# A two-layer network on one core: the second mixer's attention gets a fourth buffer of weights, and its first head's weights are scaled by a product of two tensors

## The reference, cut to what matters

```python
p = masked_softmax(jnp.einsum('bqghd,bgqkd->bghqk', qb, kg) * scale, mask)     # selected
p = masked_softmax(jnp.einsum('bqghd,bkgd->bghqk', qb, kb) * scale, mask)      # window
o = gate[..., 0:1] * heads(o_cmp) + gate[..., 1:2] * heads(o_sel) + gate[..., 2:3] * heads(o_win)
return (o.reshape(B, S, NSA_INNER) * jax.nn.silu(z)) @ w_out
```

## Time and profile before

| | |
|---|---|
| median of 3 runs | 1896.23 us |
| profiled execution, its own time | 1899.72 us |
| its span | 1898.0 us |
| busy: PE, PE's weight loads | 1824.1 us (96%), 1484.7 us (78%) |
| busy: DVE, ACT, POOL | 1095.2 us, 675.3 us, 308.9 us |
| attention stage in the trace | from 626.1 to about 775.6 us |

### The profile page before, as it was taken

The page is one execution under the profiler, slowest core; times in us unless marked ns, Lnnn a source line. Parts: engine busy times, 40 slices in busy tenths (PEclk is TensorE's granted clock), DMA queues, the critical chain, the costliest instruction groups (busy, mean ns, idle before and its releaser), DMA issues. The chain is left out here.

```text
span 1898.0 us, 36850 instructions
## 1 busy us (share of the span) xinstructions
PE 1824.1 (96%) x15870; PEld 1484.7 (78%) x15870; DVE 1095.2 (58%) x1644; ACT 675.3 (36%) x1100; POOL 308.9 (16%) x292
## 2 busy tenths in 40 slices
PE   8999999999999788999999899999999999999997
PEld 6877757688888567778888669888878888888886
DVE  4664354553257788444366887778574635354545
ACT  4334332332223577442222374433233322122342
POOL 4210011130002565320021240000001000000011
PEclk9999999999999899999999999999999999999998
DMA  5334323142223010134421100002042322322221
GB/s 191 103 111 134 136 83 133 45 190 101 90 74 111 35 37 12 49 109 138 137 102 56 48 2 4 4 3 70 4 178 92 104 104 89 111 89 89 78 100 45
DMA packets 42848, 160.87 MB, mean 85 GB/s; under 512 B 5312, under 2 KB 14528, under 8 KB 28096
## 3 DMA queue, kind: packets, MB, share of 16 engines
q1 hardware_dynamic: 28480, 143.84, 22.1%
q10 hardware_dynamic: 14208, 14.68, 2.2%
HBM read 140.42 MB, written 16.78 MB: 83 GB/s over the span
## 5 line engine op out<-in xcount | busy, mean ns | idle before, releaser
L257 DVE TENSOR_TENSOR wlo<-raw,whi 128x2048 fp32r<-128x2048 f32 (+2 forms) x113 | 251.0, 2221 | 179.2 <-ACT whi L248 178.8
L248 ACT ACTIVATE whi<-raw 128x2048 fp32r<-128x2048 f32 (+2 forms) x113 | 209.0, 1850 | 320.8 <-PE ps L283 161.4
L281 PE MATMUL ps<-act_hi,whi 128*128 128x512 f32 x616 | 243.1, 395 | 0.0
L301 PE MATMUL ps<-act_lo,whi 128*128 128x512 f32 x632 | 242.7, 393 | 0.0
L283 PE MATMUL ps<-act_hi,wlo 128*128 128x512 f32 x616 | 240.6, 391 | 0.0
L282 PE MATMUL ps<-act_lo,whi 128*128 128x512 f32 x616 | 240.5, 390 | 0.0
L300 PE MATMUL ps<-act_hi,whi 128*128 128x512 f32 x592 | 236.4, 399 | 0.0
L305 PE MATMUL ps<-act_hi,wlo 128*128 128x512 f32 x632 | 156.5, 389 | 0.0
L301 PEld LDWEIGHTS ps<-act_lo,whi 128*128 128x128 f32 x632 | 120.2, 190 | 25.9 <-issue 1.2
L305 PEld LDWEIGHTS ps<-act_hi,wlo 128*128 128x128 f32 x632 | 118.6, 188 | 24.7
L300 PEld LDWEIGHTS ps<-act_hi,whi 128*128 128x128 f32 x592 | 111.6, 188 | 32.5 <-issue 8.2
(11 more groups left out here) (550 smaller groups left out, 3474.7 us busy)
## 6 DMA issues: line engine op xcount, KB each, us to landing
raw<-stream_in SPq DMA_DIRECT2D x107, 1024.0 KB, 4.9
v_scratch<-v_out ACTq DMA_DIRECT2D x16, 256.0 KB, 3.5
z_scratch<-zt ACTq DMA_DIRECT2D x16, 256.0 KB, 2.9
mlh_v<-v_scratch SPq DMA_DIRECT2D x4, 1024.0 KB, 4.8
mlh_z<-z_scratch SPq DMA_DIRECT2D x16, 256.0 KB, 2.6
cmp_w<-cmp_w_in SPq DMA_DIRECT2D x2, 2048.0 KB, 11.3
z_scratch<-in_zt ACTq DMA_DIRECT2D x16, 256.0 KB, 3.2
mix_g<-z_scratch SPq DMA_DIRECT2D x16, 256.0 KB, 6.6
```

What stands on the lines that cost most here:

```text
L248: act.activation(k.whi[b % 2][:, 0:n], k.raw[b % RAW_SLOTS][:, 0:n], ACT.Copy).then_inc(k.hi_done, 1)
L257: dve.tensor_tensor(k.wlo[b % 2][:, 0:n], k.raw[b % RAW_SLOTS][:, 0:n], k.whi[b % 2][:, 0:n].bitcast(F32), ALU.subtract).then_inc(k.lo_don ...
L281: pe.matmul(bank, hi, x_hi, start=(x == 0), stop=False)
L301: pe.matmul(bank, hi, x_lo, start=False, stop=False)
```

## The change

Five edits go together. (1) `att_p` becomes a ring of `DEEP` = 4 buffers. (2) PE transposes unit n-3 in iteration n in place of n-2, the values are multiplied on odd n, and the copies of ACT and DVE move with them. (3) POOL scales head 0 by `tensor_tensor` with the column of the weights repeated L times (stride 0), in place of `tensor_scalar`. (4) The fourth buffer lies where the high part of the queries of pairs 2 and 3 was; this moves to a slot of the stream of weights that is free during the attention. (5) These two pairs' queries are no longer split by ACT and DVE in the projection (`None` in `high_at`), but by POOL at the start of the attention. `COPIES` is a name for what stood there as a number; the new branch for i ≥ `COPIES` on ACT is never taken, since i = 3 goes the other way.

```diff
-    high_at = (17, 18, 23, 23, 24, 24, 25, 25)
+    high_at = (17, 18, 23, 23, None, 24, None, 25)
...
-    p = k.region("att_p", [P, 3, 2, S], F32, 16)
+    DEEP, COPIES = 4, TT - 1
+    p = k.region("att_p", [P, DEEP, 2, S], F32, 16)
...
+            for t in (2, 3):
+                high(t)
+                low(t)
             for m in range(U):
                 L = length(m)
                 pool.wait_ge(s["w_done"], m + 1)
-                pool.tensor_scalar(p[:, m % 3, 0, 0:L], p[:, m % 3, 0, 0:L], sm(32, m)[:, 0:1], None, ALU.mult) \
-                    .then_inc(s["scaled0"], 1)
+                x = p[:, m % DEEP, 0, 0:L]
+                pool.tensor_tensor(x, x, sm(32, m)[:, 0:1].to_broadcast([P, L]), ALU.mult).then_inc(s["scaled0"], 1)
...
-            for n in range(U + 3):
+            for n in range(U + DEEP):
                 if n + 1 < U:
                     scores(n + 1)
-                if 2 <= n < U + 2:
-                    m = n - 2
+                if DEEP - 1 <= n < U + DEEP - 1:
+                    m = n - DEEP + 1
...
-                if n >= 4 and n % 2 == 0:
-                    c = n // 2 - 2
+                if n > DEEP and n % 2:
+                    c = (n - DEEP) // 2
...
-                        if n >= 3:
-                            act.wait_ge(s["tr_mm"], n - 2)
+                        if n >= DEEP:
+                            act.wait_ge(s["tr_mm"], n - DEEP + 1)
```

More of the change, by code:

```diff
@@ L1409, in stage_nsa_in @@
     k.gate_rows = k.region("nsa_gates", [48, S], F32, 32)
-    k.q_hi = [k.region(f"nsa_q_hi{i}", [P, 2, S], F32R, at) for i, at in enumerate((62.5, 28))]
+    k.q_hi = [k.region("nsa_q_hi0", [P, 2, S], F32R, 62.5), k.at("nsa_q_hi1", [P, 2, S], F32R, 60 + 8 * (b1 % RAW_SLOTS))]
     k.q_lo = k.region("nsa_q_lo", [P, 8, S], F32R, 0)
@@ L1687, in score_low @@
                 whole, hi, lo = parts(n)
-                dve.wait_ge(s["score_hi"], n + 1)
+                dve.wait_ge(s["score_hi"], 1 + sum(at is not None for at in high_at[:n]))
                 dve.tensor_tensor(lo, whole, hi.bitcast(F32), ALU.subtract)
@@ L1766, in _ @@
                 for n in range(8):
-                    if high_at[n] == t - 1:
+                    if high_at[n] is not None and high_at[n] == t - 1:
                         score_low(n)
@@ L1807, in copied @@
         eng.wait_ge(s["pt1"], m + 1)
-        own = sum(i < TT - 1 for _, i, _ in units[:m + 1])
+        own = sum(i < COPIES for _, i, _ in units[:m + 1])
         if own:
@@ L1828, in low @@
             def low(t):
-                pool.wait_ge(s["q_hi"], t - 3)
+                pool.wait_ge(s["q_hi"], t - 1)
                 pool.tensor_tensor(k.q_lo[:, t, :], k.q[:, t, :], query_high(t).bitcast(F32), ALU.subtract) \
                     .then_inc(s["q_lo"], 1)
+            for t in (2, 3):
+                high(t)
+                low(t)
             for m in range(U):
@@ L1865, in scores @@
                                   start=(half == 0), stop=False, skip_group_check=True)
-                if t >= 4:
-                    pe.wait_ge(s["q_lo"], t - 3)
+                if t >= 2:
+                    pe.wait_ge(s["q_lo"], t - 1)
                 at, x = slice(i * P, (i + 1) * P), t // 4
@@ L1891, in _ @@
                                 rows, at = rows_half(half), (TT * e + j) * P // 2
-                                last = pe.transpose(k.ps[:, 4 + half, at:at + P // 2], p[rows, m % 3, e, j * P:(j + 1) * P],
+                                last = pe.transpose(k.ps[:, 4 + half, at:at + P // 2], p[rows, m % DEEP, e, j * P:(j + 1) * P],
                                                     k.const("ident")[rows, rows])
                     last.then_inc(s["tr_mm"], 1)
-                if n >= 4 and n % 2 == 0:
-                    c = n // 2 - 2
+                if n > DEEP and n % 2:
+                    c = (n - DEEP) // 2
                     u = c // 2
@@ L1925, in high @@
                     act.activation(k.act_hi[:, 4 * gp + 2 * e + x, :], y[:, x, e, :], ACT.Copy).then_inc(s["y_hi"], 1)
-            for n in range(U + 2):
+            for n in range(U + DEEP - 1):
                 if n < U:
@@ L1933, in _ @@
                     for e in range(2):
-                        if n >= 3:
-                            act.wait_ge(s["tr_mm"], n - 2)
-                        act.activation(p[:, n % 3, e, 0:L], k.ps[:, 2 * (n % 2) + e, 0:L], ACT.Exp,
+                        if n >= DEEP:
+                            act.wait_ge(s["tr_mm"], n - DEEP + 1)
+                        act.activation(p[:, n % DEEP, e, 0:L], k.ps[:, 2 * (n % 2) + e, 0:L], ACT.Exp,
                                        bias=sm(0, n)[:, e:e + 1],
                                        accum_out=sm(8, n)[:, e:e + 1]).then_inc(s["exp_done"], 1)
-                if n >= 2:
-                    m = n - 2
+                if n >= DEEP - 1:
+                    m = n - DEEP + 1
                     L = length(m)
@@ L1949, in _ @@
                     else:
+                        if units[m][1] >= COPIES:
+                            out, src = turned(m, 0)
+                            act.activation(out, src, ACT.Copy)
                         out, src = turned(m, 1)
@@ L1968, in low @@
                     dve.tensor_tensor(k.act_lo[:, tile, :], y[:, x, e, :], k.act_hi[:, tile, :].bitcast(F32), ALU.subtract)                         .then_inc(s["y_lo"], 1)
-            for n in range(U + 4):
+            for n in range(U + DEEP + 1):
                 if n < U:
@@ L1978, in _ @@
                         .then_inc(s["nm_done"], 1)
-                if n >= 7 and n % 4 == 3:
-                    u = (n - 7) // 4
+                if n >= 8 and n % 4 == 0:
+                    u = (n - 8) // 4
                     t, i, _ = units[4 * u]
@@ L2002, in _ @@
                     L = length(m)
-                    dve.tensor_scalar(p[:, m % 3, 1, 0:L], p[:, m % 3, 1, 0:L], sm(32, m)[:, 1:2], None, ALU.mult) \
+                    dve.tensor_scalar(p[:, m % DEEP, 1, 0:L], p[:, m % DEEP, 1, 0:L], sm(32, m)[:, 1:2], None, ALU.mult) \
                         .then_inc(s["scaled1"], 1)
-                if 2 <= n < U + 2 and units[n - 2][1] < TT - 1:
-                    m = n - 2
+                if DEEP - 1 <= n < U + DEEP - 1 and units[n - DEEP + 1][1] < COPIES:
+                    m = n - DEEP + 1
                     L = length(m)
```

2 lines of the change are left out of this document (removed).

## The result

The changed kernel takes 1916.45 us, the median of 4 runs (1913.28 to 1917.88). The kernel before, in the same comparison, takes 1897.79 us. The ratio is 1.009, with a 95% interval from 1.0072 to 1.0107. The forecast was 1893.2 us with a range to 1898.5, so the prediction was wrong, in sign too; what happened is its rival D. Two of the later kernels have one execution each far outside the rest (2289.15 and 3638.23 us), which the ratios leave out. The profiled execution took 1915.14 us, 15.4 more than the one before.

A forecast was written before the change was run, and what follows sets the result against it. No engine is full in the attention; PE and DVE, both near it, hand each unit to one another. Terms sum to -2.98, rounded to -3.0 us: the median 1896.2 becomes 1893.2 us, range 1887.5 to 1898.5.

The forecast's parts named there:

- rival D: In the attention, POOL's new product takes the memory before DVE's scaling, which waits for all of it: +24 us; chance 0.09.
- POOL's operation: POOL's scaling of head 0 as a product: 1.47 us for 512 elements, hidden by the extra unit, so 0.
- Transposes one unit later: PE's attention transposes: all 9 waits for POOL go, 6.2 us at most, of which 2.98 us come off the end.
- C: Attention: PE reaches score banks sooner, waits there for exponentials, moved work costs 1.9 us: from -1 to +2; chance 0.23.
- Work of PE that moves: Attention: long transposes move to where PE is nearly full, at most +1.9 us, taken as even with DVE's waits: 0.
- Two splits less: Projection: two splits fewer on ACT and DVE, about 0.6 us each, taken as covered: 0, at most -1.2 us.
- Four more instructions on POOL: Start of the attention: four added POOL instructions, 5.1 us at most, end by 631.2 us, about its first scaling: 0.
- The moved buffer: Queries' buffer moved into a slot of the weights' stream: addresses only, no transfer comes later: 0.

## Why the prediction was wrong

The step that failed is *POOL's operation*. It priced the new scaling at 1.47 us on POOL, "with the same 0.43 us of standing still", and at 0 on the path. Its own work was sized rightly: 1040 ns for 512 elements, from the row of another stage with a repeated operand, 1038. What was wrong is who stands still. Not POOL for 0.43 us, but DVE for 0.87 us, and DVE had no time to spare: 30.78 of 35.80 us.

The mechanism was known and written down as rival D, with 9 in 100. Its argument against itself, "the order of the starts does not depend on POOL's operation", was true word for word (0.04 us against 0.06) and beside the point: the memory goes by when an instruction asks for it, and that moment is not in the trace. The same held the warning: DVE's product of two columns that started 0.01 us behind a `tensor_tensor` of POOL stood still, whereas the only case of DVE ahead was ahead of a `tensor_scalar`, the operation that was to go. The prediction drew "nothing changes" from a recorded lead of 0.06 us and the rule that the first to issue has the memory. The runs bear out the rule, but not that the recorded lead tells who is first.

D's size: 47 us in all (64 times 0.7 us is 45), half of it hidden, +24 us. Measured: 35.7 us on DVE, and on the end 15.4 us in the profiled execution, 18.7 us between the medians. The mean was put at 0.7 us a unit, with DVE waiting for all of POOL's time; it was 0.56, since DVE's own recorded time runs beside the first part of POOL's. About half was hidden indeed.

*Transposes one unit later*, -2.98 us: the waits for POOL went, the gain did not come. The kernel with POOL's old operation, which has all other parts of the change, stands at 0.9994. Its interval reaches from -2.9 to +0.4 us: it ends just short of the forecast's -2.98 and holds no gain at all. The sum of PE's waits (23.5 against 23.8 us) and the length of the stage in the trace (150.1 against 149.9 us) speak for C. (C's upper end is +2 in its own line and +2.3 in the range; nothing hangs on it.)

*Work of PE that moves*, 0: PE's waits for the score banks grew from 11.4 to 14.2 us in that same kernel, a sign of it that stays inside the bounds given.

*Two splits less*, 0, at most -1.2 us: probably too low. The projection's last tile on DVE starts at 620.49 (621.78 before), and PE's first scores' weights at 625.18 (626.22). That is 1.0 us, the bound rather than the value taken. The kernels with three buffers, which keep the splits, start at 626.1 to 627.6; those with four at 624.5 to 625.2, but for the one in which POOL waits for DVE's scaling: it starts at 626.9, though its added wait comes only behind this point. So some 1 us is what six traces show and one doesn't. The change also drops a wait of ACT in the projection (for `tr`, ahead of the split of a query that is gone); it was not tried apart.

```profile
620.49 0.68 DVE L1760 TENSOR_TENSOR nsa_zt<-ps,norm_nsa_root 128x512 f32<-128x512 f32 x1
```

*Four more instructions on POOL*, 0: they ran from 625.07 to 628.94, and POOL then waited 1.18 us for DVE before its first product at 630.12. *The moved buffer*, 0: nothing in the profile after speaks against it; not tried apart.

## What to carry to other kernels

Before an operation on one of POOL and DVE is exchanged, list what the other runs at that moment on SBUF: a shorter operation there can cost the neighbour its whole duration, and the bill shows up as a longer instruction on an engine whose code did not change. A recorded lead of some hundredths of a microsecond is no lead; make the order certain, by a semaphore, by a small instruction ahead, or by giving both pieces to one engine. The first two only gave back the time of before; both pieces and the small product on POOL, with four buffers, gave 0.2% more. More depth in a ring pays only where what it hides is late: worth nothing that could be measured here while DVE was near full, and about 5 us once POOL's long product was what PE waited for.

## What the runs showed of the hardware

- Between DVE's `tensor_scalar` and POOL's product, 0.04 us decide over 0.9 us: with recorded leads of DVE of 0.04 and 0.08 us the times of 512 elements are 1.37 and 1.04 us against 0.49 and 1.30 (DVE and POOL).
- On POOL a scaling by a scalar read from a column takes 1873 ns for 512 elements and a product with that column repeated 1040. Up to 0.43 us of the 1873 can be waiting for DVE's scaling beside it, which leaves 1.44, an estimate. Section 4.1 (Engine selection) of the Trainium skill's "GPSIMD Engine Reference" compares POOL with DVE: about two times slower with two inputs, near line rate with one. The first agrees (the subtraction of 512 elements takes 1.27 us on POOL and 0.68 on DVE), the second doesn't for this scaling (493 ns on DVE). Against the prediction's reading of it, POOL's product with a repeated column is shorter than its scaling by a scalar. One product of 1024 elements takes 1914 ns, of 128×256 elements 612.
- DVE's reciprocal of one column takes 164 ns where that of two takes 155: at this size the elements cost nothing that shows.
